# Experts of a two-block network in units of 64 and 32 places, with weight blocks loaded in two halves

## Chip, cores and metric

The kernel runs on one core of one Trainium2 chip. The metric is the device time of one execution in microseconds. Everything is fp32.

## The reference, cut to what matters

Two blocks follow each other on one sequence of 256 tokens and 1024 features. The first has a layer of dilated attention with a gated scan and a layer of a gated scan alone. The second has two layers, each with a mixer and a feed-forward part; in the first layer that part is dense, in the second it is the mixture of experts that the change is about:

```python
D_MODEL, SEQ, FFN_DIM, N_EXPERTS, TOP_K = 1024, 256, 3584, 8, 2

def swiglu(h, w1, w3, w2):
    return (jax.nn.silu(h @ w1) * (h @ w3)) @ w2

def moe_ffn(h, w_router, w1, w3, w2):
    logits = (h @ w_router).astype(jnp.float32)
    top_val, top_idx = lax.top_k(logits, TOP_K)
    top_w = jax.nn.softmax(top_val, -1)
    combine = jnp.sum(jax.nn.one_hot(top_idx, N_EXPERTS) * top_w[..., None], -2)
    out = jnp.zeros_like(h)
    for e in range(N_EXPERTS):
        out = out + combine[..., e:e + 1] * swiglu(h, w1[e], w3[e], w2[e])
    return out
```

A token goes to two of eight experts. The weights of one expert are 3 x 1024 x 3584 floats, 44 MB; of all eight, 352 MB.

## The kernel before, in words

Each engine runs its own program and waits on semaphores. All large weights pass through RING, seven slots of 128 partitions x 4096 floats (2 MB each). The SP queue issues the loads in the order in which TensorE uses them, one transfer of 2 MB per slot. Before it loads item n it waits until `item_used` says that TensorE is done with the item seven before, which had the same slot.

The expert stage works in turns. The router (`dve_router`, lines 2309 to 2386) ranks the experts by their number of tokens. Turn r takes the expert of rank r (called which = 0) with room for 128 tokens, its places, and the one of rank 7 - r (which = 1) with room for 64 (`CAP`, line 249). If no expert has more tokens than its places, four turns do; else another four run. All turns are one loop with a register as its count (`turn_count`, lines 2389 to 2392): each engine reads it from memory before the loop.

A turn has a prologue that is done at the end of the turn before (for turn 0, ahead of the loop): `dve_select` builds a 0/1 matrix that picks the tokens, `gather_piece` (L2408 to 2418) multiplies X with it on TensorE in three pieces through one PSUM bank, and ScalarE copies each piece with scale and bias into HTG (`act_gathered`, L2438). Then seven groups g of 512 hidden features follow (`pe_moe_turn`, L2518 to 2596). In each TensorE does, for the 128-place expert, gate and up (L2532, 8 contraction chunks of 128 features, 512 columns each) and the down of the group before (L2553); for the 64-place expert gate and up (L2535, where its 64 places stand as weights on two column groups of the array and each group streams half of the 512 columns) and down (L2555, two column groups with 512 columns each). An fp32 matmul shows as two instructions. ScalarE applies silu (L2602), VectorE multiplies (L2640), TensorE transposes the product (L2542) and ScalarE copies it to SBUF as weights of the down (L2610). The six weight blocks of a group, gate, up and down of both experts, are six items of the ring; 42 items make a turn (`turn_items`, L250 to 256; loads at L2790 to 2800).

At the end of a turn ScalarE copies both outputs (L2632, L2633). In the next turn, behind the gates of groups 0 to 3, `scatter_piece` (L2420 to 2425) multiplies them with the weighted, transposed selection, one matmul of 128 rows and one of 64, and VectorE adds the result into ACC (L2430). In turn 0 the four scatters add zeros, for which `dve_router` clears YG and SELT. After the last turn four more scatters bring the last rows, and the result is added to X and stored (L2808).

SP reads the turn count and all eight ranks into registers before its first expert load (L2785 to 2788).

Of the kernel before, what the change touches and what calls it, by code (L numbers as in the profile page):

```python
# [123 lines left out]
def network(nc, I, const_f, const_m, const_hot, const_times, out, upto=9):  # L124
    ctx = ExitStack()
    with ctx:
# [127 lines left out]
        turn_items += [(which, "down", GROUPS - 1) for which in range(2)]  # L254
# [555 lines left out]
        def pe_first(pe):  # L810
# [12 lines left out]
            pe.wait_ge(sem("padded"), 1)  # L823
# [40 lines left out]
        def act_first(act):  # L864
# [29 lines left out]
            for d in range(2):  # L894
                act.wait_ge(sem("gate_abs"), d + 1)
                act.activation(z_log[d], z_log[d], ACT.Exp)
            act.drain()
            for d in range(2):
                act.activation(z_log[d], z_log[d], ACT.Ln, bias=1.0).then_inc(sem("gate_log"), 1)
# [30 lines left out]
        def dve_first(dve):  # L930
# [8 lines left out]
            for d in range(2):  # L939
# [6 lines left out]
                dve.scalar_tensor_tensor(z_log[d], gla_g[d], -1.0, gla_g[d], ALU.mult, ALU.min).then_inc(sem("gate_abs"), 1)  # L946
            for d in range(2):
                dve.wait_ge(sem("gate_log"), d + 1)
                dve.scalar_tensor_tensor(gla_g[d], gla_g[d], 0.0, z_log[d], ALU.min, ALU.subtract)
# [82 lines left out]
        def act_second(act):  # L1032
            act.wait_ge(sem("lower_diff"), 1)
            act.activation(lb, lower[:, 0, :], ACT.Exp).then_inc(sem("lower_exp"), 1)
            for g in range(3):
# [10 lines left out]
                act.wait_ge(sem("forget"), 2 * g + 1)  # L1046
                act.activation(c_g[0], c_g[0], ACT.Ln).then_inc(sem("forget_log"), 1)
                take(act, C_GROUP[g][1], c_g[1], func=ACT.Exp, scale=-1.0, cols=S, tokens=False)
                act.wait_ge(sem("forget"), 2 * g + 2)
                act.activation(c_g[1], c_g[1], ACT.Ln).then_inc(sem("forget_log"), 1)  # L1050
# [26 lines left out]
        def dve_second(dve):  # L1077
            take_turned(dve, HT, KC)
            dve.tensor_tensor(lower[:, 0, :], lower[:, 0, :], lower[:, 1, :], ALU.subtract)\
                .then_inc(sem("lower_diff"), 1)  # L1080
            dve.wait_ge(sem("lower_exp"), 1)
# [7 lines left out]
            def forget(g, d):  # L1089
# [10 lines left out]
                dve.tensor_scalar(c_k[d], f, -1.0, 1.0, ALU.mult, ALU.add).then_inc(sem("forget"), 1)  # L1100
# [14 lines left out]
            for g in range(3):  # L1115
# [7 lines left out]
                dve.wait_ge(sem("forget_log"), 2 * g + 2)  # L1123
# [53 lines left out]
        TURN_COLS = N_EXP + 1  # L1177
# [6 lines left out]
        turns_l = keep(1)  # L1184
# [13 lines left out]
        def by_head(a):  # L1198
# [51 lines left out]
        HTG = [EX[:, 0:1024].rearrange("p (k s) -> p k s", k=KC), EX[:, 1024:1536].rearrange("p (k s) -> p k s", k=KC)]  # L1250
        ACTED = [ROW[:, 0:512], ROW[:, 512:768]]
        HIDT = [ROW[:, 1024:1536].rearrange("p (q s) -> p q s", q=4),
                ROW[:, 1536:1792].rearrange("p (a b s) -> p a b s", a=2, b=2)]
        YG = [MODB[:, 0:1024], MODB[:, 1024:1536]]
        SEL = [FREE[:, 256 * k:256 * k + 256].rearrange("p (t q) -> p t q", t=NT) for k in range(2)]
        SELW = [FREE[:, 512 + 256 * k:768 + 256 * k].rearrange("p (t q) -> p t q", t=NT) for k in range(2)]
        SELT = FREE[:, 1024:1536].rearrange("p (k t q) -> p k t q", k=2, t=NT)
# [114 lines left out]
        def dve_positions(dve):  # L1372
# [23 lines left out]
            dve.drain().then_inc(sem("angles"), 1)  # L1396
            need(dve, "sines")

        def act_positions(act):
            need(act, "angles")  # L1400
            for k in range(2):
                act.activation(trig[k], trig[k], ACT.Sin)
            act.drain().then_inc(sem("sines"), 1)
# [884 lines left out]
        def pe_router(pe):  # L2288
# [4 lines left out]
            mm.then_inc(sem("logits"), 1)  # L2293
            need(pe, "chosen")
# [6 lines left out]
            mm.then_inc(sem("places"), 1)  # L2301
            need(pe, "places_taken")

        def act_router(act):
            need(act, "top_diff")
            act.activation(top_w[:, :, 1], top_w[:, :, 1], ACT.Exp)
            act.drain().then_inc(sem("top_exp"), 1)

        def dve_router(dve):
            need(dve, "logits")  # L2310
# [9 lines left out]
            dve.drain().then_inc(sem("top_diff"), 1)  # L2320
# [8 lines left out]
            dve.drain().then_inc(sem("chosen"), 1)  # L2329
            need(dve, "top_exp")  # L2330
# [532 lines left out]
```

## Time and profile before

| | us |
|---|---|
| median of 3 runs | 2697.43 |
| lowest, highest | 2693.28, 2698.03 |
| the profiled execution | 2684.5 |
| its span, first to last instruction | 2682.6 |
| mean granted TensorE clock | 0.978 |

The router ends near 1670 us of the span; the expert stage runs from there to the end. PE is TensorE's matmuls, PEld its weight loads (they overlap PE), DVE VectorE, ACT ScalarE, SPq the queue from which SP issues transfers. A name such as L2532 is a line of the kernel. In a window, 1.00 in the column PEclk is the full TensorE clock of 2.4 GHz, 0.50 is 1.2 GHz; the DMA share is the mean busy share of 16 DMA engines, and can read a little over 1 where their packets overlap. The chain in order of time gives, for each piece, its start, its length and the number of instructions.

### The profile page before, as it was taken

To read this page: it belongs to the slowest core of one execution; us is meant where nothing else is said; L and a number is where in the kernel's file an instruction comes from. 1 tells how busy PE (TensorE), PEld (TensorE's weight loads), DVE (VectorE), ACT (ScalarE), POOL (GpSimd) and SP (SyncE) were. 2 spreads that over 40 slices of the span, in tenths; PEclk is the share of its full clock that TensorE was granted. 3 is DMA by queue.
4 is the path that set the end of the run, shared out by engine and by line. 5 is a ranking of instruction groups with operands and counts; after the bars stand their busy time and mean duration, and the time that the engine had idled before them with its cause. 6 is when DMAs were issued, how large, how long until landed. Compare 5 with 4: busy or idle time off the path is not lost.

```text
span 2682.6 us, 31497 instructions
## 1 busy us (share of the span) xinstructions
PE 2565.7 (96%) x13454; PEld 1547.2 (58%) x13454; DVE 612.2 (23%) x1435; ACT 476.1 (18%) x996; POOL 48.2 (2%) x67
## 2 busy tenths in 40 slices
PE   7998999989999999999999996999999999999998
PEld 5754787548665567776866554544444444454444
DVE  1241655633544210000254333000000000000001
ACT  1220233322215110000322331100100010010001
POOL 2300000000000000000000000000000000000000
PEclk9999999999989999999999997999999999999999
DMA  8634633355232255434533311999999989998991
GB/s 253 119 126 143 218 130 134 134 178 168 96 127 94 94 220 188 149 133 145 186 95 140 129 63 48 392 393 391 342 353 380 393 316 366 380 381 310 370 391 73
DMA packets 258218, 586.28 MB, mean 219 GB/s; under 512 B 14592, under 2 KB 16720, under 8 KB 258080
## 3 DMA queue, kind: packets, MB, share of 16 engines
q1 hardware_dynamic: 254304, 576.93, 59.0%
q0 software_dynamic: 3376, 5.94, 1.3%
q8 instruction: 112, 1.84, 0.3%
q10 hardware_dynamic: 400, 1.36, 0.2%
q14 instruction: 26, 0.21, 0.0%
HBM read 583.14 MB, written 1.06 MB: 218 GB/s over the span
## 4 chain that ended last, share of the span: by engine, by line
PE 94%; DVE 2%; DMA 2%; ACT 1%; issue 1%; DVEq 0%; ACTq 0%; SPq 0%
PE PSB L2532 15%; PE PSA L323 14%; PE PSA L338 10%; PE PSB L2535 7%; PE PSA L2553 7%; PE PSB L2473 7%; PE PSA L2555 4%; PE PSA L2455 4%; PE PSA L697 3%; PE PSA L1900 2%; PE PSB L2416 2%; PE PSA L1277 2%; PE PSA L1851 1%; PE PSB L1875 1%; PE PSB L1469 1%; PE PSB L1742 1%
## 5 line engine op out<-in xcount | busy, mean ns | idle before, releaser
L323 PE MATMUL PSA<-RING,HT 128*128 128x512 f32 (+1 forms) x896 | 395.9, 592 | 8.6 <-ACT Y L1440 5.0
L2532 PE MATMUL PSB<-RING,Y 128*128 128x512 f32 x896 | 396.8, 599 | 3.4 <-issue 3.4
L2532 PEld LDWEIGHTS PSB<-RING,Y 128*128 128x128 f32 x896 | 168.2, 192 | 213.0 <-issue 213.0
L338 PE MATMUL PSA<-HT,RING 128*128 128x256 f32 x1216 | 275.2, 387 | 9.2 <-DMA RING<-in_w_in_ab 4.3
L323 PEld LDWEIGHTS PSA<-RING,HT 128*128 128x128 f32 x896 | 167.2, 193 | 185.2 <-issue 180.0
L338 PEld LDWEIGHTS PSA<-HT,RING 128*128 128x128 f32 x1216 | 233.7, 194 | 44.3 <-issue 11.8
L2473 PE MATMUL PSB<-HT,RING 128*128 128x256 f32 x896 | 199.8, 382 | 2.0 <-DMA RING<-in_w_dense 2.0
L2535 PE MATMUL PSB<-RING,Y 128*64 128x256 f32 x1792 | 199.6, 381 | 0.0
L2553 PE MATMUL PSA<-RING,ROW 128*128 128x512 f32 x448 | 196.8, 593 | 0.0
L2473 PEld LDWEIGHTS PSB<-HT,RING 128*128 128x128 f32 x896 | 171.6, 192 | 36.8 <-issue 12.4
L2640 DVE TENSOR_TENSOR ROW<-ROW,PSB 128x512 f32<-128x512 f32 (+1 forms) x56 | 31.1, 555 | 660.4 <-ACT ROW L2602 356.6
L2535 PEld LDWEIGHTS PSB<-RING,Y 128*64 128x64 f32 x1792 | 126.2, 137 | 67.7 <-issue 7.1
L2553 PEld LDWEIGHTS PSA<-RING,ROW 128*128 128x128 f32 x448 | 85.0, 190 | 105.0 <-issue 105.0
L2610 ACT ACTIVATE ROW<-PSA 128x512 f32<-128x512 f32 (+1 forms) x56 | 27.5, 491 | 433.7 <-PE PSA L2542 433.7
L2555 PE MATMUL PSA<-RING,ROW 128*64 128x512 f32 x448 | 104.3, 609 | 0.0
L2455 PE MATMUL PSA<-RING,PROJ 128*128 128x512 f32 x224 | 100.5, 593 | 0.0
L2602 ACT ACTIVATE ROW<-PSB 128x512 f32<-128x512 f32 (+1 forms) x56 | 27.4, 490 | 394.3 <-PE PSB L2535 221.3
L2430 DVE TENSOR_TENSOR PROJ<-PROJ,PSB 128x512 f32<-128x512 f32 x20 | 13.8, 688 | 290.7 <-PE PSB L2424 290.7
L2492 DVE TENSOR_TENSOR PROJ<-PROJ,PSB 128x256 f32<-128x256 f32 x28 | 11.8, 421 | 277.1 <-PE PSB L2473 277.1
L2455 PEld LDWEIGHTS PSA<-RING,PROJ 128*128 128x128 f32 x224 | 42.7, 190 | 42.0 <-issue 40.6
L697 PE MATMUL PSA<-RING,HT 128*128 128x512 f32 x128 | 61.3, 635 | 5.1 <-ACT HT L381 5.1
L2416 PE MATMUL PSB<-HT,X 128*128 128x128 f32 (+1 forms) x320 | 45.7, 308 | 20.1 <-DVEq L284 11.4
(446 smaller groups left out, 2345.9 us busy)
## 6 DMA issues: line engine op xcount, KB each, us to landing
RING<-in_w_moe SPq DMA_DIRECT2D x168, 2048.0 KB, 11.9
RING<-in_w_ada SPq DMA_DIRECT2D x24, 2048.0 KB, 8.1
RING<-in_w_dense SPq DMA_DIRECT2D x21, 2048.0 KB, 12.1
RING<-in_w_in SPq DMA_DIRECT2D x20, 2048.0 KB, 12.3
RING<-in_w_in_c SPq DMA_DIRECT2D x15, 2048.0 KB, 8.0
RING<-in_w_in_ab SPq DMA_DIRECT2D x10, 2048.0 KB, 17.2
RING<-in_w_out SPq DMA_DIRECT2D x4, 2048.0 KB, 7.7
RING<-in_w_out_ab SPq DMA_DIRECT2D x3, 2048.0 KB, 7.8
```

What stands on the lines that cost most here:

```text
L323: mm = pe.matmul(PSA[:, lane[k], 512 * t:512 * t + cols], HT[:, c, P * t:P * t + P], W[:, c, 0:cols], start=(c == 0), stop=(c == KC - 1))
L338: mm = pe.matmul(PSA[:, lane[k], S * j:S * j + S], W[:, c, P * j:P * j + P], HT[:, c, :], start=(c == 0), stop=(c == KC - 1))
L697: mm = pe.matmul(PSA[:, t, 512 * hf:512 * hf + 512], YT4[:, c, P * t:P * t + P], W[:, c, 512 * hf:512 * hf + 512], start=(first and c == 0 ...
L1277: mm = pe.matmul(PSA[r:r + 32, lane[k], 512 * a:512 * a + 512], cT[:, c:c + 1].broadcast_to([P, 32]), W[:, c, :], start=(c < 4), stop=(c > ...
L1900: mm = pe.matmul(PSA[:, t, 512 * hf:512 * hf + 512], YMT[:, 4 * n + c, P * t:P * t + P], W[:, c, 512 * hf:512 * hf + 512], start=(n == 0 a ...
L2416: mm = pe.matmul(PSB[:, MISC, cap * i:cap * i + cap], X[:, t, P * c:P * c + P], SEL[which][:, t, 0:cap], start=(t == 0), stop=(t == NT - 1))
L2455: mm = pe.matmul(PSA[:, t, 512 * hf:512 * hf + 512], HID[k % 2][:, P * t:P * t + P], W[:, q, 512 * hf:512 * hf + 512], start=(k == 0), sto ...
L2473: mm = pe.matmul(PSB[:, 2 * which + k % 2, 0:S], W[:, c, P * q:P * q + P], HT[:, c, :], start=(c == 0), stop=(c == KC - 1))
L2532: mm = pe.matmul(UP if up else GATE, HTG[0][:, c, :], W[:, c, :], start=(c == 0), stop=(c == KC - 1))
L2535: mm = pe.matmul(BOTH[64 * j:64 * j + 64, 256 * up:256 * up + 256], HTG[1][:, c, :], W[:, c, 256 * j:256 * j + 256], start=(c == 0), stop= ...
L2553: mm = pe.matmul(OUT[0][:, 512 * hf:512 * hf + 512], HIDT[0][:, q, :], cols, start=start, stop=stop)
L2555: mm = pe.matmul(OUT[1][64 * hf:64 * hf + 64, :], HIDT[1][:, q % 2, q // 2, :], cols, start=start, stop=stop)
```

## The change

- An expert's places are cut into units. `WIDE` = 64 places of both experts of a turn are computed together: rows 0 to 63 of a PSUM tile belong to the expert of which = 0, rows 64 to 127 to the other, each fed by its own weight block. What the first expert has over 64 places is an extra of `EXTRA` = 64 places in turn 0 and 32 in the others; it stands on two or four column groups, each streaming a half or a quarter of the 512 columns. The rooms are so 128 and 64 in turn 0 and 96 and 64 in the others, and if they don't do, twelve turns run.
- Turn 0 is straight code ahead of the loop, without scatters, and reads the turn count after it. Its gather uses four PSUM banks; later gathers use one, in three pieces of up to three chunks.
- Every weight block is loaded as two transfers of 1 MB, of half its rows each, with a semaphore each: pairs of blocks go as first half of both, then second half of both. TensorE waits for the second half only at the fifth chunk (third in a down). The blocks' order in a group is gate of both, up of both, down of both. Both downs are computed in one `down`.
- SP waits for the ranks alone, reads two of them and issues the first six blocks, then reads the rest and the turn count.
- The two results of a turn are copied by ScalarE and VectorE, one each; the scatter is two matmuls of 128 rows.
- Some semaphores are shared under new names elsewhere in the kernel (`act_input`, `act_output`), and one of GpSimd became a drain.

```diff
-        CAP = (P, P // 2)
+        ROUNDS = 3
+        WIDE = P // 2
+        EXTRA = (P // 2, P // 4)
...
         for g in range(GROUPS):
-            for which in range(2):
-                turn_items += [(which, "gate", g), (which, "up", g)] + ([(which, "down", g - 1)] if g else [])
+            turn_items += [(1, "gate", g), (0, "gate", g), (1, "up", g), (0, "up", g)]
+            turn_items += [(1, "down", g - 1), (0, "down", g - 1)] if g else []
...
+            def first_wide(kind, g):
...
+                for c in range(KC):
+                    if c % 4 == 0:
+                        for which in (1, 0):
+                            load((which, kind, g), c // 4)
+                    for which in range(2):
+                        mm = pe.matmul((UP if up else GATE)[WIDE * which:WIDE * which + WIDE, :],
+                                       HTG[:, c, WIDE * which:WIDE * which + WIDE], W[which][:, c, :], start=(c == 0), stop=(c == KC - 1))
                 mm.then_inc(sem("item_used"), 1)
+            def first_extra(kind, g):
...
+                for c in range(KC):
+                    for j in range(parts):
+                        mm = pe.matmul(BOTH[ec * j:ec * j + ec, c0:c0 + pw], HTG[:, c, P:P + ec], W[:, c, pw * j:pw * j + pw],
+                                       start=(c == 0), stop=(c == KC - 1))
+                mm.then_inc(sem("item_used"), 1)
...
             for g in range(GROUPS):
+                first_wide("gate", g)
+                if g < SCATTERS and begun:
                     misc(g)
+                elif g == SCATTERS:
+                    misc(g)
+                first_extra("gate", g)
+                first_wide("up", g)
+                first_extra("up", g)
+                turned(0, g)
+                if g == GROUPS - 1:
+                    misc(SCATTERS + 1)
                 if g:
+                    down(g - 1)
+                turned(1, g)
+            misc(SCATTERS + 2)
+            down(GROUPS - 1)
+            misc(SCATTERS + 3)
...
                     for piece in range(GATHERS):
-                        if piece:
-                            pe.wait_ge(sem("misc_free"), piece)
-                        gather_piece(pe, piece).then_inc(sem("misc"), 1)
+                        gather_piece(pe, piece, EXTRA[0], piece).then_inc(sem("misc"), 1)
+                    pe_moe_turn(pe, 0)
                     n_turns = turn_count(pe)
-                    with pe.Fori(0, n_turns) as turn:
+                    with pe.Fori(1, n_turns) as turn:
                         pe_moe_turn(pe, turn)
...
+                for a, b in zip(some[::2], some[1::2]):
+                    for half in range(2):
+                        for j in (a, b):
...
+                            if half == 0:
+                                sp.wait_ge(sem("item_used"), turn * PER_TURN + (STATIC + j - SLOTS + 1))
+                            sp.dma_start(to, src).then_inc(sem(f"expert_half{half}_loaded{j % SLOTS}"), 16)
...
+            sp.wait_ge(sem("ranked"), 1)
+            for r in (0, N_EXP - 1):
+                load_rank(r)
+            load_items(0, range(SLOTS - 1))
+            for r in range(1, N_EXP - 1):
+                load_rank(r)
+            n_turns = turn_count(sp)
+            load_items(0, range(SLOTS - 1, PER_TURN))
```

## Rows read from the trace of the kernel before

**Rows 1.** The page, part 1: busy us, share of the span and instructions.
```profile
...
PE 2565.7 (96%) x13454; PEld 1547.2 (58%) x13454; DVE 612.2 (23%) x1435; ACT 476.1 (18%) x996; POOL 48.2 (2%) x67
...
```

**Rows 2.** The page, part 2: DMA share and GB/s in 40 slices of 67 us.
```profile
...
DMA  8634633355232255434533311999999989998991
GB/s 253 119 126 143 218 130 134 134 178 168 96 127 94 94 220 188 149 133 145 186 95 140 129 63 48 392 393 391 342 353 380 393 316 366 380 381 310 370 391 73
...
```

**Rows 3.** The page, part 4: chain that ended last, by engine.
```profile
...
PE 94%; DVE 2%; DMA 2%; ACT 1%; issue 1%; DVEq 0%; ACTq 0%; SPq 0%
...
```

**Rows 4.** Windows: stretch, length, busy PE, PEld, DVE, ACT, POOL, PEclk, DMA share, GB/s.
```profile
...
1700.00:1900.00 200.00, 200.00 (x844) 96.27 (x844) 11.39 (x24) 12.37 (x25) 0.00 (x0) 1.00 1.04 394
1900.00:2120.00 220.00, 217.16 (x945) 106.75 (x942) 11.82 (x25) 21.50 (x46) 0.00 (x0) 1.00 0.97 360
1667.80:2625.00 957.20, 944.66 (x3961) 464.89 (x3962) 51.01 (x108) 86.78 (x186) 0.00 (x0) 0.99 0.99 369
2160.00:2180.00 20.00, 18.63 (x73) 10.18 (x72) 0.00 (x0) 7.07 (x17) 0.00 (x0) 0.83 0.72 266
...
```

**Rows 5.** Chain in order of time, one group g of turn 0.
```profile
...
1750.98 1.05 PE PSB L2424 x2
1752.04 7.07 PE PSB L2532 x16
1759.10 6.87 PE PSA L2553 x16
1765.96 0.22 PE PSA L2542 x2
1766.18 7.06 PE PSB L2535 x64
1773.24 3.43 PE PSA L2555 x16
1776.67 0.59 PE PSA L2542 x4
...
```

**Rows 6.** Chain between turn 0 and turn 1.
```profile
...
1907.41 1.79 PE PSB L2416 x16
...
1926.81 1.46 issue
...
```

**Rows 7.** Waits of the SP queue, 1750 to 2682 us: total, times, longest.
```profile
...
SPq L2800 <- PE PSB L2532: 364.7, 51, 10.3
...
```

**Rows 8.** The page, part 6: issues of expert weights, KB, us to landing.
```profile
...
RING<-in_w_moe SPq DMA_DIRECT2D x168, 2048.0 KB, 11.9
...
```

**Rows 9.** Timeline, from the router to the first expert matmul.
```profile
...
1659.49 0.16 DVE L2355 FIND_INDEX8 small<-small 128x8 uint32<-128x8 f32 x1
...
1660.52 0.15 DVE L2366 CAST small<-small 128x1 int32<-128x1 f32 x1
...
1666.78 27.29 SPq L2800 DMA_DIRECT2D RING<-in_w_moe  x7
...
1669.53 3.78 PE L2416 MATMUL PSB<-HT,X 128*128 128x128 f32 x16 [11.37 <-DVEq L284]
...
1684.20 6.28 PE L2532 MATMUL PSB<-RING,Y 128*128 128x512 f32 x11
...
```

**Rows 10.** Chain in the second mixer: products on 64x64 tiles, 128 columns.
```profile
...
1376.14 1.91 PE PSB L1505 x64
...
```

**Rows 11.** Chain in the conditioning: 32-wide column groups, 512 columns.
```profile
...
1459.23 3.64 PE PSA L1277 x32
...
```

**Rows 12.** Windows in turn 2 and at the last load, columns as in rows 4.
```profile
...
2360.00:2380.00 20.00, 20.00 (x57) 8.78 (x54) 0.69 (x1) 1.19 (x2) 0.00 (x0) 1.00 1.03 406
2624.00:2626.00 2.00, 2.00 (x6) 0.89 (x5) 0.00 (x0) 0.00 (x0) 0.00 (x0) 1.00 0.44 164
...
```

**Rows 13.** Timeline of the last turn and the end.
```profile
...
2657.73 4.60 PE L2555 MATMUL PSA<-RING,ROW 128*64 128x512 f32 x16
...
2663.98 1.12 PE L2423 MATMUL PSB<-MODB,HT 128*128 128x512 f32 x2 [1.65 <-ACTq L284]
...
```

More of the change, by code:

```diff
@@ L1183, in network @@
         rank_key, rank_sorted, rank_i, rank_f = keep(8), keep(8), keep(8), keep(8)
-        turns_l = keep(1)
+        over = keep(3)
         turns_f = keep(1)
@@ L2427, in dve_add @@
+            return mm
         def dve_add(dve, piece, bank):
@@ L2518, in pe_moe_turn @@
         def pe_moe_turn(pe, turn):
-            def load(what):
-                j = turn_at[what]
-                pe.wait_ge(sem(f"slot_loaded{j % SLOTS}"),
-                           16 * (PER_TURN // SLOTS) * turn + 16 * (slot_loads[j % SLOTS] + j // SLOTS + 1))
-                return slot_view(j)
-            def first(which, kind, g):
-                W = load((which, kind, g))
+            ec = extra(turn)
+            parts = P // ec
+            pw = 512 // parts
+            begun = not isinstance(turn, int)
@@ L2527, in first, with load @@
+            def load(what, half):
+                j = turn_at[what]
+                pe.wait_ge(sem(f"expert_half{half}_loaded{j % SLOTS}"), 16 * (PER_TURN // SLOTS) * turn + 16 * (j // SLOTS + 1))
+            def first_wide(kind, g):
+                W = [slot_view(turn_at[(which, kind, g)]) for which in range(2)]
                 up = kind == "up"
+                if up and g:
+                    pe.wait_ge(sem("moe_turned_taken0"), each(turn, g - 1))
                 if g == 0 and not up:
-                    pe.wait_ge(sem("misc_free"), pieces(turn, which - 1))
+                    pe.wait_ge(sem("misc_free"), pieces(turn, 0 if begun else SCATTERS))
@@ L2543, in turned, with down @@
                 mm.then_inc(sem(f"moe_turned{which}"), 1)
-            def down(which, g):
-                W = load((which, "down", g))
-                pe.wait_ge(sem(f"moe_turned_taken{which}"), each(turn, g))
+            def down(g):
+                W = [slot_view(turn_at[(which, "down", g)]) for which in range(2)]
+                pe.wait_ge(sem("moe_turned_taken0"), each(turn, g))
                 for q in range(4):
+                    if q % 2 == 0:
+                        for which in (1, 0):
+                            load((which, "down", g), q // 2)
@@ new lines, in down @@
+                mm.then_inc(sem("item_used"), 1)
+                pe.wait_ge(sem("moe_turned_taken1"), each(turn, g))
+                hid = HIDT[1][:, 0:pw * ec * parts // P].rearrange("p (b j s) -> p b j s", j=parts, s=ec)
+                for b in range(pw // P):
+                    for hf in range(2):
+                        for j in range(parts):
+                            q = (pw // P) * j + b
+                            mm = pe.matmul(OUT[1][ec * j:ec * j + ec, 512 * hf:512 * hf + 512], hid[:, b, j, :],
+                                           W[0][:, q, 512 * hf:512 * hf + 512], start=(g == 0 and b == 0),
+                                           stop=(g == GROUPS - 1 and b == pw // P - 1))
@@ L2635, in dve_moe_turn @@
+                take_hidden(1, g)
+            take_misc(SCATTERS + 2)
+            act.wait_ge(sem("item_used"), used(turn, (0, "down", GROUPS - 1)))
+            act.activation(YG[0], OUT[0], ACT.Copy).then_inc(sem("moe_rows"), 1)
+            take_misc(SCATTERS + 3)
         def dve_moe_turn(dve, turn):
+            pw = 512 * extra(turn) // P
+            begun = not isinstance(turn, int)
             def hidden(which, g):
-                dve.wait_ge(sem(f"moe_silu{which}"), each(turn, g))
@@ L2642, in dve_moe_turn @@
+                dve.tensor_tensor(ACTED[which][:, 0:n], ACTED[which][:, 0:n], up, ALU.mult).then_inc(sem("moe_hidden1" if which else "hidden"), 1)
             for g in range(GROUPS):
-                if g < 4:
+                if g < SCATTERS and begun:
                     dve.wait_ge(sem("misc"), pieces(turn, g + 1))
```

342 lines of the change are left out of this document (167 added, 175 removed).

## The prediction

> **What bounds the kernel now.** I read the page's engine totals first: TensorE is busy 96% of the span [rows 1] and the chain that ended last is 94% TensorE [rows 3]. The reader should not stop there. The slices show that in the last fifteen of forty the DMA engines are nearly full too, at 310 to 393 GB/s [rows 2], and these are the expert stage: 168 loads of 2 MB [rows 8], that is 4 turns of 42, 352.3 MB in all.
>
> So the question is which of the two sets the pace there. The windows answer it [rows 4]. In the first turn TensorE is busy in all 200 us of 1700 to 1900 and DMA moves 394 GB/s at a share of 1.04: both are full. From turn 1 on TensorE has a few idle microseconds between turns and DMA falls to 360 GB/s. Over the whole stream, 1667.8 to 2625, it is 957 us at 369 GB/s. The waits of the SP queue show why it is under 394: it stands 364.7 us waiting for the matmuls of L2532 alone to free a slot [rows 7]. TensorE sets the pace and DMA is 25 GB/s behind what it can do.
>
> The chain gives TensorE's work for one group g of a turn [rows 5]: gate and up of the 128-place expert 7.06 each, gate and up of the 64-place expert 7.06 together (64 instructions), the downs 6.87 and 3.43, the transposes 0.59 and 0.22: 32.3 us. The six loads of the same group are 12.58 MB, at 394 GB/s 31.9 us. The two are balanced to 1%; only a change that shortens TensorE's part and leaves DMA a full queue gains, and no more than DMA leaves.
>
> **The change part by part.** Durations are of the profiled execution, 2684.5 us around a span of 2682.6; the median of the three runs is 2697.4, so 12.9 us are added at the end.
>
> *Units of 64 and 32 places.* Now an expert's first 64 places and its partner's 64 run on two column groups at once, and the 65th place on are an extra: 64 places in turn 0, 32 in turns 1 to 3. Two 64-wide groups that each stream 512 columns are what L2555 does: 16 instructions in 3.43 [rows 5]. The wide gate has 32 such instructions, 6.9 us, as one 128-place gate before; so have wide up and wide down. In turn 0 the extra is the former 64-place form (7.06 for gate and up, 3.43 for down): 32.3 us per group, nothing gained. In turns 1 to 3 the extra has 64 instructions of 32 weight columns and 128 moving columns each for gate and for up, on four groups. No row has that form. Between bounds: 1.91 us, the pace of 64 instructions of 128 columns on four 64x64 tiles [rows 10], and 3.53, half of the 7.06, if only two of four overlap. I take 1.91, since 32-wide groups do run four abreast with 512 columns, 32 instructions in 3.64 [rows 11]. By that row the extra down's 16 instructions take 1.82. Sum: 2 x 7.06 + 2 x 1.91 + 6.87 + 1.82 + 0.70 of transposes = 27.3 us per group, against 31.9 for DMA. A turn: 7 x 27.3, four scatters of two matmuls, the dearer one 1.05 [rows 5], so 8.4, transposes and the next gather's 32 instructions some 5 us (16 take 1.79), about 2 us of hand-overs (1.46 where the loop turns) [rows 6]: 206 us, against 88.08 MB / 394 GB/s = 223.6. **TensorE falls behind DMA in turns 1 to 3**, with 18 us to spare in each.
>
> In the tiling the two widths alternate. The rows show a price for a change of form: 7.07 for the 16 up instructions that follow the scatter's 64-row matmul, 6.87 for the down's 16 of the same shape [rows 5], 0.2 us. The Trainium skill (TensorEngine Tiling (Array Packing), Key Properties) says that changing the tiling mode drains the TensorE; by that rule, six changes a group would cost 1.2 us at the trace's 0.2, and the 4.6 us of slack cover them.
>
> *What the loads cost.* The same bytes in 336 transfers of 1 MB instead of 168. Rows of a matrix stay 2 KB and 4 KB long. The nearest row is that of 2 MB loads queued behind each other: 394 GB/s at a full share [rows 4]. An extra fixed cost per transfer that doesn't overlap isn't seen there; from below it is nothing, from above I take 0.3 us for each of 168 more (a landing of 11.9 us against 5.3 us of its own at that rate [rows 8] shows two in flight, so most of any fixed part is hidden), 50 us. I take nothing. SP's issue and register work per transfer stays short beside 2.7 us.
>
> *Can the ring keep DMA full?* A pair of loads needs a slot of the pair three before it. Between the landing of that one and the start of the new load lie two pairs of stream, 4 x 5.3 = 21 us, so TensorE may finish a wide part up to that long after its pair landed. In step with DMA it finishes 3.5 to 7 us after. In turn 0 the lag grows by 0.4 per group, by 5 for the gather at its end and by about 2 for the turn count that TensorE now loads there: about 20 us at worst. I charge 3 us.
>
> *The start.* SP now waits for the ranks (the index at 1659.6) instead of the turn count (1660.7) and loads two registers instead of nine before its first issue. 6.1 us for nine [rows 9] is 0.68 each; the first issue moves from 1666.8 to 1661.3: **5.5 us**. The other seven loads come after twelve issues, behind a full queue. The first gather starts without the memsets (about 4 us sooner) and, in four banks, without ScalarE's turns between; it took from 1669.5 to 1684.2 [rows 9]. TensorE begins near 1675, when the first pair has landed, so this gives no further time and keeps the lag small.
>
> *The stream.* 352.3 MB / 394 GB/s = 894 instead of 957 us: **63 us**.
>
> *The end.* The last load lands by 2625 [rows 12], and TensorE is done with it 37 us later, at 2662.3 [rows 13], because seven slots were waiting for it. Now it is waiting for the load: after the last half, half of a wide down (3.4), the extra down (1.8) and 1.5 for the signal, 6.7 us: **30.6 us**. The last gather piece behind the down puts 1 us back. From the first scatter to the end, 18.6 us, nothing changes. The split of DVE and ScalarE for the two result rows runs side by side. The semaphores shared under new names, the drain on GpSimd and the two dummy scatters gone from turn 0 are worth nothing: they lie under TensorE's or DMA's work.
>
> Sum: 5.5 + 63 + 30.6 - 1 - 3 = 95 us. 2684.5 - 95 = 2589.5 for a run like the profiled one; 2697.4 - 95 = **2602**.
>
> **The rivals.**
>
> *TensorE keeps a part of the pace.* If the 32-wide gate and up overlap only by two, each turn has 7 x 2 x 1.62 = 23 us more, 229 against 223.6: 16 us in three turns, 2618. A slower clock would cost more: where TensorE stood for a gather between turns the granted clock was 0.83 over 20 us [rows 4], some of it at 1.2 instead of 2.4 GHz, and it will now stand a few microseconds in each group. At 0.83 throughout turns 1 to 3 a turn is 206 / 0.83 = 248 us, 74 us in three: 2676. Against it: 4.6 us of slack per group, and a slower clock fills the very gaps that caused it. Chance 0.1 for the two, 0.03 of it for the clock.
>
> *The halves cost throughput.* Place: the boundary between two transfers on the DMA queue. If each of the 168 added boundaries costs more than 95 / 168 = 0.57 us, all is lost; at 0.85 us it is 2602 + 143 = 2745, slower. For it: DMA is now the bound, so nothing hides this. Against it: 394 GB/s through some 38 boundaries of turn 0. The Trainium skill (SBUF — State Buffer, The DMA setup-cost knee) bids one coalesce into the largest transfer and gives 341 GB/s at 1 MiB; by it the stream would be 1033 us and the time 2741, an estimate of that page. The trace's 2 MB loads, at 394, are already better than the page's curve would have them, since they queue. Chance 0.05.
>
> *The change does not take hold, or takes more turns.* If a second expert had over 96 tokens, twelve turns would run: eight more of 224 us, 4394. The reference's router on these inputs gives 102, 84, 67, 60, 58, 54, 47 and 40 tokens, which fit 128, 96 and 64. Or DMA starves on the ring after all and the pace stays as it was: the 63 us of the stream are not won, 2665. Chance 0.04 together.
>
> **How the numbers follow.** Forecast 0.81, rivals 0.1, 0.05, 0.04. A measurement of this kernel can tell about 0.2%, 5 us, from no change. The low end takes DMA at 406 GB/s, the pace of the window 2360 to 2380 [rows 12]: 868 us for the stream, 26 less, 2576. The high end takes in the 50 us for the halves, 2652, and the first half of the first rival with it: 2655. Faster by over 0.2%: 0.92; within: 0.02; slower: 0.06.
>
> **What would show it.** Right: DMA near 394 GB/s and full in every slice from 1662 to 2556; SP's waits for L2532 and its successor small after turn 0; TensorE waiting for halves of the ring in turns 1 to 3, busy near 90%; the last down 7 us behind the last landing; the 64 instructions of an extra gate in about 1.9 us. Wrong: a DMA share under 1.0 in turns 1 to 3, with SP waiting (the ring), or with two transfers always queued (the halves); extras of 3.5 us; a clock well under 1.

## The result, and the profile after

The changed kernel takes 2607.94 us in the median of four runs (2607.11 to 2612.16), the one before 2696.25 (2693.28 to 2698.03): a ratio of 0.9677, 95% interval 0.966 to 0.9693, 88 us faster. The forecast was 2602 with a range of 2576 to 2655. The profiled execution took 2612.16 us around a span of 2610.4.

The page's first two parts of the changed kernel:

```profile
...
PE 2466.6 (94%) x15945; PEld 1429.4 (55%) x15945; DVE 613.9 (24%) x1457; ACT 455.7 (17%) x949; POOL 48.2 (2%) x67
...
PEclk9999899998999999999899899799999999999999
DMA  8733633337224137435522521299999999999995
GB/s 254 128 129 107 232 133 137 129 105 258 70 96 162 65 118 268 159 132 183 190 80 98 190 75 59 91 392 394 395 394 394 394 394 393 390 395 389 393 392 231
...
```

TensorE is busy 99 us less than in [rows 1]. In [rows 2] DMA moved 310 to 393 GB/s in the expert stage, with a dip at each turn; now it is 389 to 395 in every full slice.

The windows of the changed kernel, columns as in [rows 4], one in turn 0, one in turn 1, one in turn 3:

```profile
...
1700.00:1900.00 200.00, 199.99 (x1160) 83.29 (x1157) 10.40 (x26) 13.21 (x27) 0.00 (x0) 1.00 1.04 394
1940.00:2120.00 180.00, 172.83 (x1543) 71.43 (x1539) 11.60 (x29) 11.66 (x26) 0.00 (x0) 1.00 1.04 394
2360.00:2560.00 200.00, 186.95 (x1590) 75.75 (x1590) 12.54 (x29) 13.83 (x30) 0.00 (x0) 0.98 1.04 391
...
```

The answer to [rows 4]: the 360 GB/s of turn 1 have become 394 at a share of 1.04, and TensorE, full in turn 0, stands still for 4% of the window in turn 1 and 7% of the one in turn 3. The pace has changed hands. The waits say the same from both sides. SP's, against 364.7 us for L2532 alone in [rows 7]:

```profile
...
SPq L2855 <- PE PSB L2556: 31.4, 15, 7.4
SPq L2855 <- PE PSB L2569: 29.1, 17, 4.5
...
```

and TensorE's, which had no wait for RING in this stage before:

```profile
...
PE PSB L2556 <- DMA RING<-in_w_moe: 25.9, 19, 2.0
...
PE PSA L2588 <- DMA RING<-in_w_moe: 3.3, 6, 0.6
...
```

The chain in order of time through a group of turn 1, with a scatter ahead (L2450), then extra gate or up (L2569), wide gate or up (L2556), transposes (L2576), wide down (L2588) and extra down (L2598):

```profile
...
1955.52 1.91 PE PSB L2450 x4
1957.43 1.89 PE PSB L2569 x64
1959.32 7.02 PE PSB L2556 x32
1966.33 1.89 PE PSB L2569 x64
1968.22 0.59 PE PSB L2576 x4
1968.80 7.02 PE PSA L2588 x32
1975.82 1.85 PE PSA L2598 x16
1977.67 0.26 PE PSB L2576
1977.93 7.02 PE PSB L2556 x32
...
```

The 64 instructions of an extra gate, a form that no row of before had, take 1.89 us. The same chain in turn 0 has the wide part behind a 64-place extra, and then behind the transposes:

```profile
...
1705.71 6.87 PE PSB L2556 x32
...
1717.06 7.02 PE PSB L2556 x32
...
```

**Where the time went.** The part ahead of the expert stage differs from execution to execution (experiment 10), so the two profiles are set side by side from the router's first instruction, MAX8 on VectorE. The table is worked out from the timelines and the DMA packets of the two profiles; a turn's end is the start of ScalarE's copy of its result (L2632 before, L2675 after).

| from MAX8, us | before | after | gain |
|---|---|---|---|
| first expert load issued | 13.3 | 8.0 | 5.3 |
| first packet to last packet of the weights | 959.9 | 903.9 | 56.0 |
| last packet to end of last down | 34.6 | 6.1 | 28.5 |
| from there to the end of the span | 20.3 | 19.6 | 0.7 |
| all, MAX8 to the end | 1029.2 | 938.7 | 90.5 |
| end of turn 0 | 273.4 | 253.1 | 20.3 |
| turns 1, 2, 3 | 246, 241, 248 | 215, 226, 225 | 31, 15, 23 |

Of the 20.3 us of turn 0, 7.3 are its earlier first expert matmul (23.5 instead of 30.8 us after MAX8); the four scatters of zeros that are left out are most of the rest, some 2 us each where a scatter of turn 1 shows in the trace of before. Turn 1 is shorter than turns 2 and 3 because it begins with a ring full of blocks: 45.5 blocks had come in 253 us after MAX8, counted from the packets, and 42 were used.

One line of this table is safer than its parts. A second profile of the kernel before (experiment 10) gives 1029.4 us in all, but 957.1 for the stream, 31.7 to the end of the last down, 26.2 from there to the end, and 243, 246 and 241 for the turns: in it the last scatters ran at a granted clock of 0.50. The parts of before are good to some 3 to 6 us, and that the totals agree to 0.2 is in part chance.

The start, from the timeline, with SP's first issue, the gather in four banks and the first expert matmul:

```profile
...
1671.70 0.24 DVE L2315 MAX8 small<-small 128x8 f32<-128x8 f32 x2
...
1679.74 19.12 SPq L2855 DMA_DIRECT2D RING<-in_w_moe  x10
...
1686.95 7.21 PE L2435 MATMUL PSB<-HT,X 128*128 128x192 f32 x32 [10.54 <-DVEq L286]
...
1695.17 2.37 PE L2556 MATMUL PSB<-RING,Y 128*64 128x512 f32 x10 [1.00 <-ACT Y L2442]
...
```

The end, from the timeline: the last matmuls that wait for a load (the second half of the last wide up), the down of the group before (wide, then extra), a gather piece, the last wide down, the last extra down, the scatters and the store of the result:

```profile
...
2563.45 3.65 PE L2556 MATMUL PSB<-RING,Y 128*64 128x512 f32 x16 [1.64 <-DMA RING<-in_w_moe]
...
2571.14 7.09 PE L2588 MATMUL PSA<-RING,ROW 128*64 128x512 f32 x32
...
2578.16 1.92 PE L2598 MATMUL PSA<-RING,ROW 128*32 128x512 f32 x16
...
2580.18 1.80 PE L2435 MATMUL PSB<-HT,X 128*128 128x160 f32 x12
...
2581.90 7.09 PE L2588 MATMUL PSA<-RING,ROW 128*64 128x512 f32 x32
...
2588.92 1.92 PE L2598 MATMUL PSA<-RING,ROW 128*32 128x512 f32 x16
...
2593.11 7.13 PE L2450 MATMUL PSB<-MODB,HT 128*128 128x512 f32 x16 [0.98 <-ACTq L286]
...
2605.96 0.39 SPq L2878 DMA_DIRECT2D result<-X  x1
```

### The profile page after: what moved, and what is told of

Its sections match the earlier page's. It is cut to its first block, busy times and chain, and to the rows that moved or that the text cites. A ratio compares the mean times of both kernels' runs of the same rounds, so it can differ in the third digit from the quotient of the medians.

```text
span 2610.4 us, 36900 instructions
## 1 busy us (share of the span) xinstructions
PE 2466.6 (94%) x15945; PEld 1429.4 (55%) x15945; DVE 613.9 (24%) x1457; ACT 455.7 (17%) x949; POOL 48.2 (2%) x67
## 4 chain that ended last, share of the span: by engine, by line
PE 83%; DMA 7%; SPq 5%; DVE 2%; ACT 1%; issue 1%; DVEq 1%; ACTq 0%
PE PSA L325 15%; PE PSA L340 10%; PE PSB L2556 10%; PE PSB L2489 7%; DMA RING<-in_w_moe 6%; PE PSA L2588 6%; SPq L2855 4%; PE PSA L2471 4%; PE PSB L2569 3%; PE PSA L699 3%; PE PSA L1278 2%; PE PSA L1901 2%; PE PSA L2598 2%; PE PSA L1852 1%; PE PSB L1470 1%
## 5 line engine op out<-in xcount | busy, mean ns | idle before, releaser
L2556 PE MATMUL PSB<-RING,Y 128*64 128x512 f32 x1792 | 405.3, 601 | 35.2 <-DMA RING<-in_w_moe 25.9
L2556 PEld LDWEIGHTS PSB<-RING,Y 128*64 128x64 f32 x1792 | 128.7, 138 | 272.8 <-issue 268.3
L2588 PE MATMUL PSA<-RING,ROW 128*64 128x512 f32 x896 | 200.0, 596 | 3.3 <-DMA RING<-in_w_moe 3.3
L2686 DVE TENSOR_TENSOR ROW<-ROW,PSB 128x512 f32<-128x512 f32 (+2 forms) x56 | 28.2, 504 | 583.4 <-PE PSB L2556 546.2
L2569 PE MATMUL PSB<-RING,Y 128*32 128x128 f32 (+1 forms) x3136 | 132.9, 289 | 0.0
L2569 PEld LDWEIGHTS PSB<-RING,Y 128*32 128x32 f32 (+1 forms) x3136 | 102.8, 114 | 53.3 <-issue 39.1
L2588 PEld LDWEIGHTS PSA<-RING,ROW 128*64 128x64 f32 x896 | 62.8, 137 | 120.6 <-issue 120.6
L2655 ACT ACTIVATE ROW<-PSB 128x512 f32<-128x512 f32 (+2 forms) x56 | 25.1, 450 | 499.2 <-PE PSB L2576 498.9
L2647 ACT ACTIVATE ROW<-PSB 128x512 f32<-128x512 f32 (+2 forms) x56 | 25.2, 450 | 284.5 <-PE PSB L2556 213.8
L1278 PE MATMUL PSA<-RING,small 128*32 128x512 f32 x384 | 59.7, 778 | 11.8 <-DVE X L709 5.0
L2598 PE MATMUL PSA<-RING,ROW 128*32 128x512 f32 (+1 forms) x448 | 65.6, 597 | 0.0
L353 ACT ACTIVATE PROJ<-PSA 128x1024 f32<-128x1024 f32 x33 | 33.7, 1020 | 158.7 <-PE PSA L340 80.6
```

Source lines behind the costliest of these rows:

```text
L1278: mm = pe.matmul(PSA[r:r + 32, lane[k], 512 * a:512 * a + 512], cT[:, c:c + 1].broadcast_to([P, 32]), W[:, c, :], start=(c < 4), stop=(c > ...
L2556: mm = pe.matmul((UP if up else GATE)[WIDE * which:WIDE * which + WIDE, :], HTG[:, c, WIDE * which:WIDE * which + WIDE], W[which][:, c, :] ...
L2569: mm = pe.matmul(BOTH[ec * j:ec * j + ec, c0:c0 + pw], HTG[:, c, P:P + ec], W[:, c, pw * j:pw * j + pw], start=(c == 0), stop=(c == KC - 1))
L2588: mm = pe.matmul(OUT[0][WIDE * which:WIDE * which + WIDE, 512 * hf:512 * hf + 512], HIDT[0][:, g % 2, q, WIDE * which:WIDE * which + WIDE] ...
L2598: mm = pe.matmul(OUT[1][ec * j:ec * j + ec, 512 * hf:512 * hf + 512], hid[:, b, j, :], W[0][:, q, 512 * hf:512 * hf + 512], start=(g == 0 ...
```

## The experiments

Each run is compared with runs of the kernel before on the same chip. Beside the median stands the time from MAX8 to the end in the profile of the run, "the stage". It leaves out the part ahead, which varies by up to 19 us, and so tells differences that the medians, of runs that spread by some 10 us, do not. But each is one profile; only the kernel before was profiled twice (1029.2 and 1029.4, with parts that differ by up to 6). A difference of 1 or 2 us is taken as real here only where the timeline shows the instructions that make it. In the changed kernel the stage is 938.7.

**1. Only TensorE's saving undone.**

```diff
-        EXTRA = (P // 2, P // 4)
+        EXTRA = (P // 2, P // 2)
...
-        GATHERS, TURN_GATHERS, SCATTERS = 4, 3, 4
+        GATHERS, TURN_GATHERS, SCATTERS = 4, 4, 4
...
             misc(SCATTERS + 3)
+            misc(SCATTERS + 4)
...
```

> The changed kernel with extras of 64 places in every turn, so that only the saving on TensorE is undone (the gather takes four pieces instead of three). Theory: TensorE's shorter part is what lets DMA run full. A turn on TensorE is again 7 x 32.3 + 8.4 + 10 = 244 us against 224 of DMA, so turns 1 to 3 lose 50 to 65 us: 2660 to 2673, and SP waits for TensorE again. Rival: the gain comes from the loads (halves, their order, the early start), and TensorE's part is not needed: 2605 to 2615.

2683.3 us, ratio 0.9945 (0.9921 to 0.997); stage 1014.4, turns 1 to 3 of 242, 248 and 249 us. SP's waits and the windows of turns 1, 2 and 3:

```profile
...
SPq L2857 <- PE PSB L2556: 304.7, 50, 18.2
...
```

```profile
...
1960.00:2120.00 160.00, 160.00 (x892) 64.73 (x890) 8.96 (x19) 9.81 (x20) 0.00 (x0) 1.00 1.01 374
2180.00:2340.00 160.00, 160.00 (x887) 64.94 (x885) 11.06 (x26) 10.28 (x21) 0.00 (x0) 1.00 0.95 355
2400.00:2540.00 140.00, 133.74 (x720) 55.60 (x718) 10.74 (x24) 10.91 (x22) 0.00 (x0) 0.98 0.90 332
...
```

All but 15 us of the gain is gone, with the halves, their order, the early start and the new turn 0 in place: together they give little. The order of the blocks was not undone by itself, nor was TensorE's saving tried with the old loads.

The loss of 76 us in the stage is more than the 50 to 65 expected. Turns 1 to 3 take 739 us in all against 666, where the expectation took 3 x 244 against 3 x 224, 60 us. Of the other 13, 7 are these turns, 246 on average; 6 are the changed kernel's, whose turn 1 takes 215 and not 224, since it begins with a full ring. The last 3 us lie behind the last down (22.4 instead of 19.6), where the fourth gather piece stands in the way. Seen from DMA the same 73 us are 52 of a longer stream (955.5 us) and 21 of a longer way from the last packet to the end of the last down (27 us instead of 6).

**2. TensorE relieved further.** The rest of the extra's sum in turns 1 to 3 is left out.

```diff
-                for c in range(KC):
+                chunks = 1 if begun else KC
+                for c in range(chunks):
...
-                                       start=(c == 0), stop=(c == KC - 1))
+                                       start=(c == 0), stop=(c == chunks - 1))
```

> In turns 1 to 3 the extra gate and up do only the first of their eight contraction chunks (the rest of that sum is left out), 3.3 us less TensorE work per group. Theory: DMA sets the pace there, so the time stays within 4 us of 2608, and TensorE waits more. Rival: TensorE still sets a part of it: up to 3 x 23 = 69 us less, 2540 to 2590.

2607.5 us, ratio 0.9663 (0.962 to 0.9706); stage 936.2. Windows:

```profile
...
1960.00:2120.00 160.00, 139.96 (x733) 47.97 (x729) 8.08 (x20) 9.60 (x22) 0.00 (x0) 0.99 1.04 394
2180.00:2340.00 160.00, 135.23 (x695) 45.48 (x693) 7.20 (x18) 9.01 (x21) 0.00 (x0) 0.99 1.04 394
...
```

TensorE is busy 85 to 87% of these stretches; in the same two of the changed kernel it is 93 to 96%. DMA moves the same 394 GB/s, and the time stays. 69 us less work on TensorE, by the expectation, are worth 2.5 us of the stage.

**3. DMA relieved.** The last quarter of every block of turns 1 to 3 is not loaded.

```diff
+                            if half and not isinstance(turn, int):
+                                n = to.shape[1] // 2
+                                to, src = to[:, 0:n, :], src[:, 0:n, :]
```

> In turns 1 to 3 the second half of every block moves only half of its rows, so 12 instead of 16 MB of every 16 are loaded (part of the weights is left out, and old data stands in its place). Theory: DMA would need 168 us a turn, TensorE 206, so the turns fall from 224 to the 206 of the prediction: 45 to 55 us less, 2553 to 2563, with TensorE fully busy. Rival: TensorE is at its own bound already, or its real work is longer than 206: the time stays above 2590.

2563.8 us, ratio 0.9498 (0.9455 to 0.954), 0.8 us above what the theory expected; the turns take 207.4, 207.6 and 207.6 us. Windows:

```profile
...
1960.00:2120.00 160.00, 160.00 (x1395) 65.47 (x1392) 8.53 (x20) 11.44 (x26) 0.00 (x0) 1.00 0.89 326
2180.00:2340.00 160.00, 158.41 (x1340) 64.36 (x1338) 7.48 (x13) 13.96 (x31) 0.00 (x0) 1.00 0.89 325
...
```

This measures what the other bound hid: TensorE's own turn, forecast as 206, is 207.5 us, DMA's is 225.5. The gap of 18 is the one that the prediction gave. (DMA's turn was forecast as 223.6; 225.5 is the mean of turns 2 and 3 of the changed kernel, where TensorE waits for DMA.)

**4. Whole blocks.** One transfer of 2 MB per block, in the same order.

```diff
...
+                if half:
+                    return
-                    for half in range(2):
+                    for half in range(1):
...
+                            to = slot_view(j)
...
-                                src = w[:, 512 * g + 256 * half:512 * g + 256 * half + 256, :].rearrange("a (k p) n -> p (a k) n", p=P)
-                                to = slot_view(j)[:, 2 * half:2 * half + 2, :]
+                                src = w[:, 512 * g:512 * g + 512, :].rearrange("a (k p) n -> p (a k) n", p=P)
...
```

> One transfer of 2 MB per block again, in the same order. Theory: the stream runs at the same pace, and only the last down starts later, since it waits for whole blocks: 2 to 6 us more, 2610 to 2614. Rival 1: the halves cost throughput, and whole blocks win it back: 0.3 us for each of 168 transfers would be 50 us less, 2558. Rival 2: the halves carry a good part of the gain, because TensorE can't keep in step with whole blocks: 2625 or more.

2609.7 us, ratio 0.9672 (0.9638 to 0.9706); stage 942.1, 3.4 more. The full slices show 388 to 396 GB/s. The halves neither cost throughput (the stream takes 902.3 us here, 903.9 with halves) nor carry the gain. The expectation's size was right, its place wrong: the last down, which begins at 2582.08, does not wait for its blocks, whose last packet is at 2579.9. The last wait for a load is ahead of the last wide up, 891.8 us after MAX8. In the changed kernel the wait that ends 891.8 us after MAX8 stands in the middle of that part, 3.65 us of which are left; here all 7.09 are. That is the 3.4 us.

**5. Quarters.** Each half as two transfers, 672 in all, with the same semaphore counted to 32.

```diff
-                pe.wait_ge(sem(f"expert_half{half}_loaded{j % SLOTS}"), 16 * (PER_TURN // SLOTS) * turn + 16 * (j // SLOTS + 1))
+                pe.wait_ge(sem(f"expert_half{half}_loaded{j % SLOTS}"), 32 * (PER_TURN // SLOTS) * turn + 32 * (j // SLOTS + 1))
...
-                            sp.dma_start(to, src).then_inc(sem(f"expert_half{half}_loaded{j % SLOTS}"), 16)
+                            n = to.shape[1] // 2
+                            for part in range(2):
+                                sp.dma_start(to[:, n * part:n * part + n, :], src[:, n * part:n * part + n, :])\
+                                    .then_inc(sem(f"expert_half{half}_loaded{j % SLOTS}"), 16)
```

> Each half is loaded as two transfers of 512 KB: 672 transfers instead of 336, the suspected cost per transfer twice more. Theory: queued transfers overlap their fixed part, so the time stays within 5 us of 2608. Rival: a price per transfer; at 0.3 us for each of 336 it is 100 us more, 2708, and the DMA rate in full slices falls below 394 GB/s.

2611.9 us, ratio 0.9682 (0.9658 to 0.9706); stage 939.5. Windows:

```profile
...
1960.00:2120.00 160.00, 153.23 (x1302) 62.56 (x1300) 6.24 (x12) 10.83 (x25) 0.00 (x0) 1.00 1.04 395
2180.00:2340.00 160.00, 147.62 (x1259) 60.34 (x1257) 6.24 (x12) 10.57 (x24) 0.00 (x0) 1.00 1.04 393
...
```

The stage with 336 more transfers is 0.8 us longer, which a second profile might not repeat; even taken as real it is 2 ns each. A transfer of this size has no price here as long as another is queued behind it.

**6. Longer rows.** Gate and up blocks as 512 rows of 4 KB from other places of the matrix: the bytes are the same, the numbers are not those of the reference.

```diff
-                                src = w[:, 512 * half:512 * half + 512, 512 * g:512 * g + 512].rearrange("a (k p) n -> p (a k) n", p=P)
-                                to = slot_view(j)[:, 4 * half:4 * half + 4, :]
+                                c0, r0 = min(1024 * (g // 2), 2560), 512 * (g % 2) + 256 * half
+                                src = w[:, r0:r0 + 256, c0:c0 + 1024].rearrange("a (k p) n -> p (a k) n", p=P)
+                                to = slot_view(j).rearrange("p (a x) b -> p a (x b)", x=2)[:, 2 * half:2 * half + 2, :]
```

> Gate and up blocks are fetched as 512 rows of 4 KB instead of 1024 rows of 2 KB, the same bytes from other places (the weights land in the wrong arrangement, so the products are of other numbers). Theory: DMA is the bound in turns 1 to 3, so its pace shows in the time: 28 of a turn's 42 blocks at the pace of the down blocks, about 412 instead of 388 GB/s, give 8.8 us a turn in turns 1 to 3, 2575 to 2588 if turn 0 gains nothing. Rival: the time is not set by DMA's pace: 2605 to 2610.

2586.2 us, ratio 0.9591 (0.9567 to 0.9615); stage 913.1, 25.6 less against 26 expected. Windows:

```profile
...
1960.00:2120.00 160.00, 160.00 (x1344) 64.35 (x1344) 6.24 (x12) 12.06 (x28) 0.00 (x0) 1.00 1.03 409
2180.00:2340.00 160.00, 154.04 (x1309) 63.41 (x1305) 7.47 (x13) 13.66 (x30) 0.00 (x0) 1.00 1.03 409
...
```

A faster stream goes straight into the time: DMA is the bound. Its rate here is 409 GB/s with rows of 4 KB against 394 for the mix of 2 and 4 KB; the rows also come from other places of the matrix and are longer in the ring, so that the length in memory alone makes it is likely and not shown. A kernel that could use such blocks would have to hold two groups' gates and ups in PSUM at once; that wasn't tried.

**7. The old start.** SP reads the turn count and all ranks first.

```diff
-            sp.wait_ge(sem("ranked"), 1)
-            for r in (0, N_EXP - 1):
-                load_rank(r)
-            load_items(0, range(SLOTS - 1))
-            for r in range(1, N_EXP - 1):
-                load_rank(r)
             n_turns = turn_count(sp)
-            load_items(0, range(SLOTS - 1, PER_TURN))
+            for r in range(N_EXP):
+                load_rank(r)
+            load_items(0, range(PER_TURN))
```

> SP again reads the turn count and all eight ranks before its first expert load. Theory: DMA is full from its first transfer to its last, so all of the 5.3 us by which it begins later come back: 2612 to 2614. Rival: turn 0 is paced by TensorE, whose start the loads don't set, and the ring takes the delay up: 2607 to 2609.

2614.5 us, ratio 0.9692 (0.9669 to 0.9716), whose interval holds the changed kernel's. The stage tells more: 944.2, 5.5 longer, with the first issue 13.5 instead of 8.0 us after MAX8. A microsecond of start lost is a microsecond of time.

**8. The last gather piece ahead of the last down.**

```diff
             misc(SCATTERS + 2)
+            misc(SCATTERS + 3)
             down(GROUPS - 1)
-            misc(SCATTERS + 3)
...
+            take_misc(SCATTERS + 3)
             act.wait_ge(sem("item_used"), used(turn, (0, "down", GROUPS - 1)))
             act.activation(YG[0], OUT[0], ACT.Copy).then_inc(sem("moe_rows"), 1)
-            take_misc(SCATTERS + 3)
```

> The last gather piece of a turn goes ahead of the last down instead of behind it, and ScalarE copies it before the result rows. Theory: TensorE waits for loads before that down anyway, and 1.1 us of matmuls and 0.9 us of copies leave the way to the last scatter: 1 to 3 us less, 2605 to 2607. Rival: the scatter waits for the drains and not for the piece: no difference.

2608.4 us, ratio 0.9671 (0.9644 to 0.9698); stage 940.6, 1.9 longer: the expectation was wrong. TensorE in the timeline, the third gather piece of this turn, its fourth, the wide and the extra down:

```profile
...
2572.18 1.79 PE L2435 MATMUL PSB<-HT,X 128*128 128x160 f32 x12
2575.30 1.35 PE L2435 MATMUL PSB<-HT,X 128*128 128x160 f32 x8 [1.33 <-ACT Y L2442]
2576.59 7.09 PE L2588 MATMUL PSA<-RING,ROW 128*64 128x512 f32 x32
2583.61 1.92 PE L2598 MATMUL PSA<-RING,ROW 128*32 128x512 f32 x16
...
```

TensorE doesn't wait for loads ahead of the last down. It comes from the down before and the gather, and the fourth piece has to wait 1.3 us for ScalarE to empty the one bank. The last down ends 30.1 us after TensorE's last wait for a load instead of 27.4, by the piece and that wait; behind the down 0.8 us are won (18.7 instead of 19.6).

**9. Four blocks ahead of the router**, from fixed experts, so that the sums are of other weights.

```diff
...
+            sp.wait_ge(sem("item_used"), STATIC)
+            load_items(0, range(4), (0, N_EXP - 1))
             sp.wait_ge(sem("ranked"), 1)
...
-            load_items(0, range(SLOTS - 1))
+            load_items(0, range(4, SLOTS - 1))
```

> The first four blocks of the expert stage are fetched as soon as the mixer's last block is used, some 28 us before the ranks are known, and so from the fixed experts 0 and 7 (the choice by rank is left out for these four blocks, so the sums are of other weights). Theory: DMA has 21 us less to move once the ranks are known. TensorE begins no sooner and paces turn 0, so the ring bounds the gain: at the end of turn 0 DMA is now some 4 of at most 7 blocks ahead, and 3 more are 16 us: 12 to 17 us less, 2591 to 2596. Rival: the time is set by TensorE's start and DMA is only along with it: 2606 to 2610.

2604.3 us, ratio 0.9659 (0.9632 to 0.9685); stage 934.3: 4.4 less, not 12 to 17. Windows before the first expert matmul and at the end of turn 0:

```profile
...
1660.00:1680.00 20.00, 8.91 (x64) 8.53 (x63) 10.75 (x63) 3.53 (x6) 0.00 (x0) 0.67 0.85 306
1680.00:1700.00 20.00, 15.74 (x78) 10.45 (x80) 2.63 (x13) 5.54 (x10) 0.00 (x0) 0.82 0.59 220
1900.00:1940.00 40.00, 38.86 (x238) 15.95 (x236) 1.92 (x2) 4.38 (x9) 0.00 (x0) 1.00 0.94 338
...
```

The first packet comes 16.7 us ahead of MAX8 instead of 9.1 behind it, but DMA then stands in front of a full ring, at 220 GB/s until TensorE begins and 338 at the end of turn 0. The changed kernel's ring was nearly full already. Counted from the packets and issues, 253 us after MAX8, when turn 0 ends with 42 blocks used, it has 45.5 blocks landed and 47.5 issued of the 49 that fit; here they are 46.7 and 48. The expectation counted the landed blocks alone and left out that blocks under way hold slots too. Together with experiment 7: a later start costs all of itself, an earlier one by 26 us gives under 5.

**10. The kernel before once more.**

> The kernel before, unchanged, for the part ahead of the expert stage. In its first profile the router's first instruction stood at 1653 us of the span, in the changed kernel's at 1672, and in seven kernels with the same code up to there between 1660 and 1673. Theory: that part varies from execution to execution, and from the router to the end this kernel takes 1029 us again, wherever the router stands. Rival: the change made the part ahead slower: the router stands at 1653 again, within 3 us.

2697.6 us, ratio 1.0003 (0.9985 to 1.0022). The router in its timeline:

```profile
...
1671.37 0.24 DVE L2314 MAX8 small<-small 128x8 f32<-128x8 f32 x2
...
```

From MAX8 to the end it is 1029.4 us, as in the first profile (1029.2), but MAX8 stands at 1671.4 instead of 1653.4. So the part ahead varies by 18 us with the same code; the first profile of before had the quickest such part of all twelve, and its 2684.5 lie under every one of the four runs that the result is compared with.

## Why the prediction was right, step by step

**Direction and mechanism held.** TensorE set the pace, DMA was 25 GB/s behind what it can do, and with TensorE's part shortened in turns 1 to 3 DMA ran full and became the bound (experiments 1 to 3). The term for term comparison, in the stage:

- *TensorE's group in turns 1 to 3*, forecast 27.3: the chain gives 27.5 (three wide parts of 7.02, two extras of 1.89, 1.85, 0.85 of transposes), and a turn 207.5 for 206. The extra gate was taken as 1.91 between 1.91 and 3.53, by the row of 64x64 tiles; it is 1.89. Right.
- *The drains between tiling modes*, 1.2 us a group by the trace's 0.2: a wide part takes 7.02 in turn 1 behind every change of form, and 6.87 in turn 0 when it follows a 64-place extra, a difference of 0.15 us, which the slack covers. The Trainium skill says that a change of the tiling mode drains TensorE (TensorEngine Tiling (Array Packing), Key Properties); these 0.15 us agree with it.
- *The halves*, taken as nothing between nothing and 50 us: the stream takes 902.3 us with whole blocks, 903.9 with halves and 903.7 with quarters. The Trainium skill (SBUF — State Buffer, The DMA setup-cost knee) gives 341 GB/s for 1 MiB transfers, which made 2741 us, an estimate from that page. It does not hold for the transfers here, queued behind one another: 394 GB/s at 1 MB and at 512 KB.
- *The start*, 5.5 us: 5.3, and experiment 7 gives it back as 5.5. Right.
- *The stream*, 63 us: 56. This is the term whose size was furthest off: "352.3 MB / 394 GB/s = 894 instead of 957 us". Before it was 959.9 us, 3 more than read from the rows, and after it was 903.9, 10 more than the sum. The rate of 394 held in turn 0 and turn 1; the later slices show 389 to 395, and turns 2 and 3 take 225.5 us instead of 223.6. Counted from the packets against a steady 394, 1.5 of the 10 us go in the first 100 us of the stream, some 4 between there and its last 10 us, and 4.3 in these. DMA does not end at once, as the windows of the changed kernel at the last load show:

```profile
...
2574.00:2576.00 2.00, 2.00 (x12) 0.66 (x10) 0.00 (x0) 0.00 (x0) 0.00 (x0) 1.00 1.04 416
2576.00:2578.00 2.00, 2.00 (x12) 0.49 (x8) 0.00 (x0) 0.00 (x0) 0.00 (x0) 1.00 0.86 342
2578.00:2580.00 2.00, 2.00 (x18) 0.42 (x16) 0.00 (x0) 0.00 (x0) 0.00 (x0) 1.00 0.53 219
2580.00:2582.00 2.00, 2.00 (x19) 1.82 (x17) 0.00 (x0) 0.28 (x1) 0.00 (x0) 1.00 0.52 213
2582.00:2584.00 2.00, 2.00 (x10) 0.67 (x12) 0.00 (x0) 1.24 (x3) 0.00 (x0) 1.00 0.25 90
...
```

- *The end*, 30.6 us: 28.5, since the last packet before came at 2627.7 and not by 2625. After it, forecast 6.7, measured 6.1, but not in the way that was told. The prediction has TensorE "waiting for the load" at the last down. The timeline shows no matmul that waits behind the second half of the last wide up, at 2563.45, whose blocks landed at 2563.3. From there TensorE has 27.5 us of its own work to the end of the last down, and DMA needs 21.4 us for the four blocks that are left (last packet at 2584.7); the 6.1 are the difference. TensorE comes to the last half of the last down at 2585.4, 0.7 us after that packet, so the two ways are nearly equally long, and that their end fits the forecast is in part luck. Experiments 4 and 8 show the same way from the last up to the end.
- *The charges*, 1 for the gather behind the last down and 3 for a ring that runs dry: the gather costs 0.6 to 0.8 us (the first scatter begins 2.27 us behind the last down instead of 1.65, and experiment 8 wins 0.8 there). It doesn't show in the sum, because from the first scatter to the end, where the prediction said that nothing changes, it is 17.3 us instead of 18.6: the last four scatters, now all on 128 rows, take 7.13 us (L2450); with 128 and 64 rows in turn they took 8.5 before. The ring never ran dry: DMA's share is 1.04 or more in every window of 20 us through turn 0 and the hand-over.

The sum was 95, the stage gave 90.5 and the medians 88. The 6 us from 2602 to 2608 are these 4.5 and 2.2, less 1.2 by which the median of before fell with its fourth run; the 2.2 are not explained beyond the spread of the part ahead.

**The rivals.** "TensorE keeps a part of the pace" did not come: the clock was granted in full in turns 1 to 3, except for a few windows of 20 us, at 0.91 to 0.96. "The halves cost throughput" is refused by experiments 4 and 5. That more turns run is refused by the 336 transfers, that the stream gains nothing by its rate.

## What to carry to other kernels

Where two resources are within 1% of each other, shortening one gains only what the other has left, and that is to be counted over the whole stream, its start and its end: here 5 us of start and 28 us of end came beside 56 in the middle. When the pace changes hands from the engine to the loads, the ring's backlog at the end vanishes as well: 28 us here, of the 37 that seven blocks take at 394 GB/s. Once the loads set the pace, more relief for the engine (2.5 us of the stage), smaller transfers (nothing) and a start that is still earlier (4.4 us for 26) are worth little, and longer rows are worth 25 us. And a term that comes out right is not yet a mechanism that was right: where the last wait stands is read from the timeline, from its end backwards.

## What was not expected of the hardware

- At the end of a stream that has been full throughout, DMA falls to half its rate, 213 to 219 GB/s, for about 5 us before it stops. All eight kernels here whose DMA was full through turns 1 to 3 show this, over 5 to 9 us; the four in which TensorE held it up end within 1 to 4 us. Half the rate fits half of the 16 engines being done some 6 us, 0.7%, ahead of the rest. Which ones, and why they are slower, the packets don't say; this stays open. It makes some 4 of the 10 us by which the stream missed its forecast, and no time: no matmul waits for these last packets.
- The part ahead of the experts takes 1653 to 1673 us with nearly the same instructions in all twelve profiles, 1653 and 1671 with exactly the same. The lag between a quick and a slow execution grows in steps of some 3 to 5 us, most of them at the conditioning matmuls: the granted clock over 1265 to 1295 us was 1.00 in the run of experiment 5 (MAX8 at 1660.7) and 0.77 in the changed kernel's profile (1671.7). What sets it there was not tried.
